# The sample's cross-attention front moved into the mixer's last two turns, eight convolution taps of the last tile moved to TensorE, and the last tile's routing reordered

## The reference, cut to what matters

```python
q, k, v, u = mixer_projections(x, ...)            # RMSNorm, x @ w_in, QK-norm, GLU
attn = sliding window attention (window 128, 8 heads of 64, 2 KV heads, sinks)
conv = silu(layernorm(depthwise_conv(u, width 31) + dw_b))       # 512 channels
x = x + concat(attn, conv) @ w_out
# cross-attention, 4 heads of 256; the prompt shares 256 memory rows,
# each of the 8 sample sequences has its own 256 keys and values
q = rmsnorm((rmsnorm(x) @ w_mq).reshape(n, t, 4, 256), mq_norm_g)
x = x + softmax(q @ mem_k.T * 256 ** -0.5) @ mem_v @ w_mo
# MoE: 4 groups of 8 experts, top 1 group, top 2 experts in it
x = x + sum over the two experts of gate * (silu(h @ w_gate) * (h @ w_up)) @ w_down
```

## Time and profile before

| | |
|---|---|
| median of 3 runs | 1385.19 us (1384.43 to 1388.69) |
| the profiled execution | 1390.01 us, span 1387.8 us |
| TensorE busy | 1231.1 us, 89% of the span |
| VectorE busy | 715.1 us, 52% |
| ScalarE busy | 311.8 us, 22% |
| GpSimd busy | 156.8 us, 11% |
| granted TensorE clock, mean | 0.94 of full speed |
| DMA | 207.35 MB, mean 149 GB/s |

### The profile page before, as it was taken

One profiled execution on the slowest core, in us unless ns is written; L12 is line 12 of the kernel. 1 busy time (PEld: TensorE's weight loads), 2 busy tenths in 40 slices (PEclk: granted clock), 3 DMA queues, 4 the chain that ended last, 5 costly groups with the idle time before them and its releaser, 6 DMA issues. The chain is left out here.

```text
span 1387.8 us, 17739 instructions
## 1 busy us (share of the span) xinstructions
PE 1231.1 (89%) x6455; PEld 632.0 (46%) x6455; DVE 715.1 (52%) x2214; ACT 311.8 (22%) x891; POOL 156.8 (11%) x173
## 2 busy tenths in 40 slices
PE   7978979999999938687999999998759999999992
PEld 3444554555555423453555666655423433333330
DVE  2118799999999984331345554455434422222210
ACT  1134334534535341120111111111001111101100
POOL 0000000000000000100000000000012333333322
PEclk9988899999999968897999999999869999999996
DMA  8860000300000040373114200003368999999952
GB/s 319 289 211 20 0 24 0 153 31 1 31 31 16 1 149 31 140 276 122 31 46 187 86 16 31 31 31 121 144 258 328 383 360 391 376 375 378 367 155 37
DMA packets 52367, 207.35 MB, mean 149 GB/s; under 512 B 14160, under 2 KB 17142, under 8 KB 38435
## 3 DMA queue, kind: packets, MB, share of 16 engines
q1 hardware_dynamic: 39611, 186.27, 34.9%
q0 software_dynamic: 12096, 17.88, 5.5%
q10 hardware_dynamic: 576, 2.10, 0.4%
HBM read 187.17 MB, written 46.56 MB: 168 GB/s over the span
## 5 line engine op out<-in xcount | busy, mean ns | idle before, releaser
L806 PE MATMUL bank<-W,G 128*128 128x512 f32 (+1 forms) x768 | 314.0, 564 | 3.7 <-DVE G L1656 2.9
L1712 DVE SCALAR_TENSOR_TENSOR W<-W,dwT 128x128 f32<-128x128 f32 (+1 forms) x1080 | 280.0, 335 | 0.0
L806 PEld LDWEIGHTS bank<-W,G 128*128 128x128 f32 x768 | 145.2, 192 | 150.5 <-issue 147.1
L1256 PE MATMUL bank<-W 128*32 128x512 f32 x1264 | 199.8, 600 | 4.1 <-issue 2.4
L1030 PE MATMUL bank<-W 128*128 128x512 f32 x256 | 116.5, 614 | 10.6 <-ACT W L1502 6.7
L2134 DVE TENSOR_TENSOR W<-bank,cvec 128x512 f32<-128x512 f32 x56 | 36.2, 686 | 164.0 <-PE bank L1243 163.9
L682 POOL TENSOR_SCALAR st<-st 128x1 f32<-128x1 f32 (+3 forms) x41 | 8.0, 196 | 935.9 <-DVE st L1795 470.1
L1205 PE MATMUL bank<-W 128*128 128x512 f32 x256 | 113.3, 595 | 0.2 <-DVE W L2021 0.2
L1256 PEld LDWEIGHTS bank<-W 128*32 128x32 f32 x1264 | 59.4, 115 | 104.1 <-issue 101.7
L1263 PE MATMUL bank<-W 128*32 128x512 f32 x632 | 101.6, 595 | 0.5 <-ACT W L1604 0.5
L1030 PEld LDWEIGHTS bank<-W 128*128 128x128 f32 x256 | 49.7, 197 | 72.1 <-issue 71.8
(11 more groups left out here) (297 smaller groups left out, 1549.1 us busy)
## 6 DMA issues: line engine op xcount, KB each, us to landing
W<-in_w_exp_gate SPq DMA_DIRECT2D x29, 1024.0 KB
W<-in_w_exp_up SPq DMA_DIRECT2D x29, 1024.0 KB
W<-in_w_exp_down SPq DMA_DIRECT2D x29, 1024.0 KB
W<-in_cache_mem_k SPq DMA_DIRECT2D x8, 1024.0 KB, 5.7
W<-in_cache_mem_v SPq DMA_DIRECT2D x8, 1024.0 KB, 7.2
W<-in_w_in SPq DMA_DIRECT2D x4, 1792.0 KB, 25.4
G<-in_w_exp_gate SPq DMA_DIRECT2D x7, 1024.0 KB
G<-in_w_exp_up SPq DMA_DIRECT2D x7, 1024.0 KB
```

The lines of the kernel that those rows point to most:

```text
L806: mm = pe.matmul(bank[0:rows, at:at + hi - lo], HT[:, c, 0:rows], w[:, c, lo:hi], start=(c == 0), stop=(c == DC - 1))
L1256: mm = pe.matmul(B[2 + par][lo:hi, :], HG[par][:, c, lo:hi], WGU[u][:, :, c, :], start=(c == 0), stop=(c == DC - 1), skip_group_check=True)
L1712: dve.scalar_tensor_tensor(y, src, w, y, ALU.mult, ALU.add).then_inc(M["conv_tap"], 1)
```

## The change

Four things.

1. The sample tile's cross-attention front moves from the first turns of the cross-attention into the mixer. Its x1 is read back early (SP, turn 7; the ring is renamed, `XB(s) = XR[(s + 3) % 4]`), squared and rooted on ScalarE and scaled on VectorE in turn 8. In turn 9 TensorE transposes Z first of all, projects by w_mq once all scores are evacuated, and VectorE sums the squares and makes QN2. In turn 10 TensorE transposes QN2 behind the mean product of tile 8, turns batch 0's keys (`turn_early(0)`), then the variance, then batch 1's keys, then the spread. QT2 and QP2 are made by VectorE between `add_x1` and the copy of the variance; all eight copies of these keys are ScalarE's. The cross-attention's loop starts at turn 1, with tile 1.
2. Of tile 8's taps, VectorE does 23 of 31. The last 8 are TensorE products of U with diagonal matrices, 4 x 8 matmuls of 128x128x128 into bank 3 in turn 9, behind the spread; ScalarE builds the 32 diagonals, 12 ahead of the exponentials and 20 behind tile 7's square; VectorE adds bank 3 to Y.
3. In the routing, the operations for the gates stand behind those for the positions, and for the last tile the table's two halves are made by separate matmuls.
4. SP issues the load of slot 5 only when the first two gathers have landed.

```diff
+DVE_TAPS = 23
+        QN2_S = view(G, 8192, MH, MHD)
+        QT2_S = HT[:, :, 0:NS]
+        DIAG = view(W, RIN + 8192, TAPS - DVE_TAPS, CC, 128)
@@ SP, mixer
-                if s3 == 6 or s3 == 7:
-                    s = s3 - 6
-                    sp.wait_ge(x1_out[s], 32)
-                    sp.dma_start(XR[s][0:rows_of(s), :], tok_rows(x1_d, s)).then_inc(x1_in[s], 16)
+                if 5 <= s3 <= 7:
+                    s = s3 - 5
+                    sp.wait_ge(x1_out[(s + 3) % 4], 32)
+                    sp.dma_start(XB(s)[0:rows_of(s), :], tok_rows(x1_d, s)).then_inc(x1_in[s], 16)
             sp.wait_ge(M["wo_done"], 2 * NT)
-            sp.wait_ge(M["x_sq"], NT + 3)
+            sp.wait_ge(M["x_sq"], NT + 4)
@@ SP, before the load of slot 5
+                    sp.wait_ge(zg_in[0], 16)
+                    sp.wait_ge(zg_in[1], 16)
@@ TensorE
+            def diagonal_taps():
+                pe.wait_ge(M["diag_ready"], CC * (TAPS - DVE_TAPS))
+                for c in range(CC):
+                    for t in range(TAPS - DVE_TAPS):
+                        tap = DVE_TAPS + t
+                        mm = pe.matmul(B[3][:, c * 128:(c + 1) * 128], DIAG[:, t, c, :], UT[(NT - 1) % 2][:, c, tap:tap + 128], start=(t == 0), stop=(tap == TAPS - 1))
+                mm.then_inc(M["fold_done"], 1)
+            def turn_early(b):
+                pe.wait_ge(mk_in[b], 16)
+                for mt in range(2):
+                    if mt == 0 and b:
+                        pe.wait_ge(M["mk0_ready"], 2)
+                    if mt == 1:
+                        pe.wait_ge(M["mk0_ready"], 4) if b else pe.wait_ge(M["q2T_ready"], AFTER["q2T_ready"] + 2)
+                    (8 transposes of MKB[b] into banks 4, 5 or 2, 3)
@@ TensorE, mixer
+                if s1 == NT:
+                    (waits) turn_z(NT + 2, NS, (5, 4))
-                elif s3 >= 0:
+                elif s1 == NT:
+                    pe.wait_ge(M["wmq_in"], 64)
+                    pe.wait_ge(M["s_ready"], 8 * NT)
+                    for mm in sample_pair((B[4], 0, 512, w_mq), (B[5], 512, 1024, w_mq)):
+                        mm.then_inc(M["mq_done"], 1)
                     ln_variance(s3)
                     ln_spread(s3)
+                    diagonal_taps()
+                else:
+                    pe.wait_ge(M["q2n_ready"], AFTER["q2n_ready"] + 2)
+                    (8 transposes of QN2_S)
+                    turn_early(0)
+                    ln_variance(s3)
+                    turn_early(1)
+                    ln_spread(s3)
@@ ScalarE
+            def build_diagonals(t0, t1):
+                for t in range(t0, t1):
+                    for c in range(CC):
+                        at = c * TAPS + DVE_TAPS + t
+                        act.activation(DIAG[:, t, c, :], ident, ACT.Copy, scale=dwT[:, at:at + 1]).then_inc(M["diag_ready"], 1)
@@ VectorE, mixer, turn 9
+                if s1 == NT:
+                    dve.wait_ge(M["q2_sq"], AFTER["q2_sq"] + 2)
+                    dve.tensor_reduce(st[0:NS, 32:36], Z[0:NS, :]...).then_inc(M["q2_ssq"], 1)
+                    conv_taps(s2, CUTS[3], CUTS[4])
+                    (waits) two products into QN2_S
-                    conv_taps(s2, CUTS[4 if s1 < NT else 3], CUTS[5])
+                    conv_taps(s2, CUTS[4], CUTS[5])
+                if s2 == NT - 1:
+                    dve.wait_ge(M["fold_done"], 1)
+                    dve.tensor_tensor(Y[s2], Y[s2], B[3][:, :]..., ALU.add)
```

More of the change, by code:

```diff
@@ L826, in ln_variance @@
                 mm.then_inc(M["ln2_done"], 1)
+            def turn_early(b):
[5 more added lines that the diff above has]
+                        pe.wait_ge(M["mk0_ready"], 4) if b else pe.wait_ge(M["q2T_ready"], AFTER["q2T_ready"] + 2)
+                    for half, done in enumerate(("mkb_tA", "mkb_tD")):
+                        for c in range(4):
+                            k = 4 * half + c
+                            mm = pe.transpose(B[(2 if mt else 4) + half][:, c * 128:(c + 1) * 128], MKB[b][:, mt, k * 128:(k + 1) * 128], ident)
+                        mm.then_inc(M[done], 1)
             def ln_spread(s3):
@@ L1097, in _ @@
                     n2 = rows_of(s2)
[L1098 removed]
                     if s2 >= 1:
+                        pe.wait_ge(M["q2n_ready"], AFTER["q2n_ready"] + 2 * s2 + 2)
                         pe.wait_ge(M["ot2A_ready"], AFTER["ot2A_ready"] + s2)
                         pe.wait_ge(M["ot2D_ready"], s2)
[L1102 removed]
+                    for half in range(2 if s2 else 0):
                         for c in range(4):
@@ L1447, in _ @@
                     act.activation(TMP[:, 0:CC * n3], Y[s3].rearrange("p c t -> p (c t)"), ACT.Square).then_inc(M["ln_sq"], 1)
+                if s2 == NT - 1:
+                    build_diagonals(3, TAPS - DVE_TAPS)
+                if s2 == NT:
+                    for b in range(2):
+                        for mt in range(2):
+                            for half, done in enumerate(("mkb_tA", "mkb_tD")):
+                                act.wait_ge(M[done], AFTER[done] + 2 * b + mt + 1)
+                                act.activation(MKTB[b][:, 4 * half:4 * half + 4, mt * 128:(mt + 1) * 128],
+                                               B[(2 if mt else 4) + half][:, :].rearrange("p (c t) -> p c t", c=4), ACT.Copy).then_inc(M["mk0_ready"], 1)
                 if 0 <= s2 < NT:
@@ L1504, in _ @@
                     squares(s1)
+                if s1 == NT:
+                    act.wait_ge(M["zt_done"], 2 * (NT + 3))
+                    for half in range(2):
+                        act.wait_ge(M["mq_done"], AFTER["mq_done"] + half + 1)
+                        act.activation(Z[0:NS, 512 * half:512 * half + 512], B[4 + half][held(0, half), :], ACT.Square).then_inc(M["q2_sq"], 1)
                 if s1 < NT:
@@ L1698, in conv_taps @@
                 base = CC * TAPS * s
-                for k in range(k0, k1):
+                for k in range(k0, min(k1, CC * DVE_TAPS) if s == NT - 1 else k1):
                     tap, c = k // CC, k % CC
@@ L1780, in _ @@
                     add_x1(s3 - 1)
+                if s2 == NT:
+                    for half in range(2):
+                        dve.wait_ge(M["q2T_done"], AFTER["q2T_done"] + half + 1)
+                        for r in range(2):
+                            c = 4 * half + 2 * r
+                            a = dve.tensor_tensor(QT2_S[:, c:c + 2, :], B[2 + half][:, 256 * r:256 * r + 256].rearrange("p (c t) -> p c t", c=2)[:, :, 0:NS],
+                                                  gain(V_MQ, 2, NS), ALU.mult)
+                        a.then_inc(M["q2T_ready"], 1)
+                    dve.wait_ge(M["qp2_zero"], 1)
+                    dve.wait_ge(M["q2T_ready"], AFTER["q2T_ready"] + 2)
+                    for b in range(DEC_B):
+                        dve.tensor_copy(QP2[:, b, :, DEC_T * (b % 4):DEC_T * (b % 4) + DEC_T], QT2_S[:, :, b * DEC_T:(b + 1) * DEC_T]).then_inc(M["qp2_ready"], 1)
                 if 0 <= s2 < NT:
@@ L1946, in route_add @@
                     dve.sem_inc(M["r_acc"], 1)
-            norm_z(NT + 2, rows_of(0), XR[0])
-            for it in range(NT + 3):
+            norm_z(NT + 3, rows_of(1), XB(1))
+            for it in range(1, NT + 3):
                 s1, s2, s3, s4 = it, it - 1, it - 2, it - 3
@@ L1956, in _ @@
                     n2 = rows_of(s2)
-                    for half in range(2):
+                    for half in range(2 if s2 else 0):
                         dve.wait_ge(M["q2T_done"], AFTER["q2T_done"] + 2 * s2 + half + 1)
```

170 lines of the change are left out of this document (104 added, 66 removed).

## The result

| | before | after |
|---|---|---|
| median of the runs beside each other | 1384.81 us (1380.79 to 1388.69, 4 runs) | 1369.36 us (1368.38 to 1371.65, 4 runs) |
| ratio | | 0.9893, 95% interval 0.9873 to 0.9913 |
| the profiled execution | 1390.01 us, span 1387.8 | 1368.40 us, span 1366.3 |
| granted TensorE clock, mean | 0.940 | 0.952 |

What follows compares the result with a forecast made beforehand. TensorE was taken to bound the cross-attention's steady turns and expert stage, key loads the scan from batch three. Terms 0 - 11.0 - 0.2 - 3.5 = -14.7 on 1385.2 gave 1370.5 us; forecast 1367 to 1374 (0.70), range 1364 to 1378.

Steps and rivals of the forecast that it cites:

- Turns 9 and 10: Mixer's last two turns: no net change, 0 us, bounds -1 and +4; mixer end at 562.8.
- The w_mq projection: Turn 9 on TensorE: 7.09 us falling into the old 8.54 us wait, so it costs nothing.
- rival D: ScalarE's 32 diagonals make it slower: hidden up to 0.5 us each, 3.2 us per 0.1 more; chance 0.04.
- the diagonal products: Turn 9 on TensorE: 32 products taking 3.81 us at full clock, 7.6 at half.
- The rest of 2.3 us: Turn 9: TensorE works from 508 to 517, then rests 2.3 us before tile 7's projection.
- The fold: Tile 8's taps moved off VectorE: worth nothing by itself, pays only for the room the front's work takes.
- After the mixer: Key scan of the cross-attention: keys load earlier, scan ends at 606 instead of 617.0, -11.0 us, bounds -14 and -8.
- Rival E: After the mixer: the change does not bring the key loads forward, 1381 to 1387 us; chance 0.03.
- Routing and gather: Expert stage's start: gates off the way -0.2 us; slot 5's load held back for the first gathers -3.5 us.
- A: The tail gives much back: projections at the lower clock, mixer end +4, slow loads; 1377.5 us, chance 0.14.
- C: Everything at the good bounds, -1 - 13 - 4.5: 1366.7 us or a little less; chance 0.09.

Runs made afterwards that it cites:

- the fold alone: The kernel before with only 8 of tile 8's taps made as diagonal products in turn 9, nothing of the front moved: 1388.02 us, ratio 1.0017.
- the keys ahead of w_mo: The changed kernel with key batches 2 and 3 loaded in turn 10 and w_mo loaded behind the last key batch: 1351.82 us, ratio 0.9774.
- the late turn: The changed kernel with the transposes and copies of key batches 0 and 1 back at the start of the cross-attention: 1371.49 us, ratio 0.9899.
- the layer norm first: On the keys ahead of w_mo: in turn 10 tile 8's variance goes before batch 0's keys, the spread before batch 1's: 1351.75 us, ratio 0.9751.
- six taps: On the layer norm first: 25 taps on VectorE and 6 as diagonal products, instead of 23 and 8: 1353.87 us, ratio 0.9756.

## Why the prediction was right

The forecast was right within 1.1 us, and the waits that it named are those that went. But the agreement is closer than its parts: the terms of the sum were put at -14.7 and came to -16.9 between the two traces; the 2.6 us that were missed behind the mixer make the difference.

**Turns 9 and 10: 0 predicted, +0.2 found, from sizes that cancelled.** Against the prediction the start of the layer norm came 0.5 late, its chain was 1.1 shorter and the last projection 0.7 longer. The w_mq projection cost nothing and ran at full clock, as put. ScalarE's diagonals took 0.30, not 0.41; rival D had its point at 0.5 and is out. The mis-sized term is the diagonal products: 3.8 to 7.6 us in the working, 9.86 in the trace. A float32 product here is two records. I divided L1183's 3.81 us by 32 products, but its 32 records are 16; and the products start at the lower level (11 records in 2 us at 508 to 510, 20 at 512 to 514). The rest of 2.3 us that I expected ahead of the projection was filled by them, so the miss of 2 to 6 us moved the projection only 0.6, to 519.7 on the scale of before (518.08 + 1.65), predicted 519.1. It took 13.97, predicted 14.0; the layer norm of tile 8 stands at 535.5, predicted 535.0. The chain behind it grew by 1.9 (11.72 against 9.82), not 3.0; tile 8's projection took 15.67, predicted 15. Mixer end 562.9, predicted 562.8. All at full clock, the 64 records would have taken 6.4 (20 in 2 us) to 7.6 us (twice L1183's 3.81). One reading of the earlier trace rows was off as well: 0.62 in the microsecond from 578 on puts the fall of the clock 4.6 us behind 573.7, not 4.9; no term used it.

**The fold: "nothing by itself, it pays only for the room".** In time that stood up (1.0017 alone, 3.7 us beside the moved front), but the reason was too narrow. Up to the layer norm, "room" on VectorE is 1.0 of it; the clock of tile 7's projection is 2.6. The prediction had the 2.5 us of clock in its sum, as a gain of turn 9 and not of the fold.

**After the mixer: -11.0 predicted, -13.6 found.** Batch 2's turn was put at 580.8 and came at 580.1 on the scale of before, behind w_mo, at the lower level (3.65; 3.40 was taken). That w_mo's four loads are what binds is shown from both sides: 10.6 us go when they move behind the keys, and nothing comes when the first two batches are turned late. From batch 2's turn to the last scores it took 23.5 us, predicted 25.2: the pairs' loads land in 5.1 (median), and no turn behind batch 2's was slow. Rival E is out.

**Not in the sum: -2.1 between the scan's end and the sample's output projection.** That projection took 9.61 before and 7.09 after; the granted clock is 0.73 over the former. In the experiments the same instructions took 7.09 three times, 8.24, 8.66, 9.21 and 9.47, with the fold alone 8.54. With one trace of each kernel it is not shown whether this goes with the kernel or with the single execution. It is 2.1 of the 4.6 us that the two traces show outside the prediction's terms.

**Routing and gather: -0.2 and -3.5 predicted, -0.1 and -3.4 found.** The experiment without the hold-back gives 3.5 in time (2.5 by the ratios). TensorE now waits only 0.77 us for the gather, since its own small product for the table ends at 1000.4; a still faster gather could bring no more than that. The new order of the routing was not taken out by itself, and 0.1 us is within what two traces differ by. Nor was the moved front run without the other three parts.

**Rivals A and C.** A (1377.5) asked for a late mixer end and slow loads; neither came. Of C (1366.7) only the part behind the mixer came. The point where I was lucky is the cancelling in turn 9.

## What to carry to other kernels

When a change moves work out of a queue's way, ask at once what the moved wait lands behind: here batch 2's keys came 14 us sooner and then stood behind 4 MB that nobody needed for over 70 us; putting the two loads in the order of use was worth more (17.5 us) than the whole change (15.4). Work moved into TensorE's rests can be worth more than its place if it ends just before a long projection, since that then runs at the full clock (13.97 us instead of 16.59 here). A gain on one chain counts only up to the next point at which a load sets the pace: of the fold's 2.35 us 1.0 was left at the end of the key scan. So follow a gain from milestone to milestone, to the end of the span, before giving it a price. Count records of a float32 product against a line whose number of products is known before dividing its duration.

## What the runs showed of the hardware that I had not expected

- The clock's level makes 1.7 to 2.9 us in one projection: 13.97, 15.67, 16.23, 16.59 and 16.87 us for the same 32 records of 128x512, 7.09 to 9.75 for the sample's. The level need not be low at the start. In the kernel after, tile 8's projection began at 545.57 behind a rest of 3.89 us at full level (1.00 from 545.0 to 545.5), ran at 0.50 from 546.0 to 549.0 and at 1.00 again from 549.5: 15.67 us.
- The expert stage stretches a slow start. Its first block has 64 records that took 8.4 to 8.5 us in four traces (the change, the keys ahead of w_mo, the late turn, the layer norm first); from the first gather's turn to the end these took 364.3 to 365.1 us. In four others (before, no hold-back, no fold, the fold alone) it was 9.1 to 9.4 and 366.0 to 367.1, in the last two (w_mo behind the keys, six taps) 9.9 to 10.0 and 368.9 to 369.1. A wait of TensorE 53 to 66 us before the end, for which the trace names no releaser, grows with it: at most 0.5 us, 2.2 to 3.2, and 3.3. The transfers' share was 1.00 from 1180 to 1280 in the kernel after. A weight stream without slack that falls behind at the start would look like this, but no run tested it. These are the 4 us that w_mo behind the keys and six taps give back at the end.
- The level rose while the diagonal products ran (0.50 until 510, 1.00 from 512), after a wait of 7.06 us and then work without a gap from 505.88 on; without the products (the fold taken out) the projection at 518.00 began at the lower level. So short products can bring the clock up ahead of a projection.
- GpSimd's root of 64x4 took 4.66 us beside VectorE's taps, 1.01 in the kernel before, where it stood after the mixer with VectorE nearly idle; it was 4.65 or 4.66 in all eight kernels with the front in the mixer and 1.01 in both without. VectorE's work beside it is not the whole cause: the root of 128x1 took 0.55 us beside the same taps at 502.88. The cause stays open. VectorE waited 0.98 us for this root at 526.27, with time to spare until TensorE's mean product. GpSimd's timeline in the kernel after, then in the kernel before:

```profile
521.51 4.66 POOL L693 TENSOR_TENSOR st<-st,mhalf 64x4 f32<-64x4 f32 x1
```

```profile
576.57 1.01 POOL L686 TENSOR_TENSOR st<-st,mhalf 64x4 f32<-64x4 f32 x1
```
